# Attention in a hybrid trunk: the row maxima are turned four query tiles at a time and placed by VectorE, and the first pass is masked inside VectorE's maximum

## The reference, cut to what matters

```python
scale = q.shape[-1] ** -0.5
for blk in range(T // Q_BLOCK):
    lo, hi = blk * Q_BLOCK, (blk + 1) * Q_BLOCK
    s = jnp.einsum('bqhd,bkhd->bhqk', q[:, lo:hi], k[:, :hi]) * scale
    if log_decay_cum is not None:                      # fox only
        s = s + (cum[:, :, lo:hi, None] - cum[:, :, None, :hi])
    mask = (lo + jnp.arange(Q_BLOCK))[:, None] >= jnp.arange(hi)[None, :]
    p = jax.nn.softmax(jnp.where(mask, s, -jnp.inf), axis=-1)
    outs.append(jnp.einsum('bhqk,bkhd->bqhd', p, v[:, :hi]))
```

## Time and profile before

| what | value |
|---|---|
| median of 3 runs | 2560.76 us (2560.36 to 2562.09) |
| the profiled execution | 2564.89 us, of it span 2563.1 us |
| mean granted TensorE clock | 0.973 of full |
| TensorE matmuls busy | 2378.3 us (93%), 14804 |
| VectorE busy | 1163.1 us (45%), 1756 |
| ScalarE busy | 917.1 us (36%), 1508 |
| GpSimd busy | 792.6 us (31%), 740 |
| DMA | 141.33 MB, 54 GB/s over the span |

### The profile page before, as it was taken

The page is one execution under the profiler, slowest core; times in us unless marked ns, Lnnn a source line. Parts: engine busy times, 40 slices in busy tenths (PEclk is TensorE's granted clock), DMA queues, the critical chain, the costliest instruction groups (busy, mean ns, idle before and its releaser), DMA issues.

```text
span 2563.1 us, 35660 instructions
## 1 busy us (share of the span) xinstructions
PE 2378.3 (93%) x14804; PEld 1818.5 (71%) x14804; DVE 1163.1 (45%) x1756; ACT 917.1 (36%) x1508; POOL 792.6 (31%) x740
## 2 busy tenths in 40 slices
PE   7988999898999999899999889989999999998998
PEld 7867877885695876555696778778756858765556
DVE  4278144624335226565423872255342451266542
ACT  4332225513334333344332322263143243334341
POOL 1264211212514520354413532211134144203452
PEclk9989999999999999999998999999999999999999
DMA  4100331230100213100311003403201002131003
GB/s 145 53 18 2 93 121 38 99 115 1 34 17 1 64 38 115 58 1 1 133 67 53 18 1 99 148 6 133 81 1 34 17 1 64 37 115 58 1 1 123
DMA packets 91873, 141.33 MB, mean 55 GB/s; under 512 B 18208, under 2 KB 65344, under 8 KB 91712
## 3 DMA queue, kind: packets, MB, share of 16 engines
q1 hardware_dynamic: 91712, 139.05, 15.8%
HBM read 105.48 MB, written 33.55 MB: 54 GB/s over the span
## 4 chain that ended last, share of the span: by engine, by line
PE 77%; DVE 15%; ACT 3%; issue 2%; POOL 1%; DMA 1%; SPq 0%; POOLq 0%; DVEq 0%; ACTq 0%
PE psum L237 32%; PE psum L491 12%; PE psum L1379 6%; PE psum L1364 4%; PE psum L1333 4%; DVE gla_A L750 3%; PE psum L1365 3%; PE psum L1367 3%; PE psum L1346 2%; PE psum L1318 2%; PE psum L729 2%; PE psum L1386 1%; PE psum L981 1%; PE psum L1766 1%; DVE mla_nm L1514 1%
## 5 line engine op out<-in xcount | busy, mean ns | idle before, releaser
L196 POOL TENSOR_TENSOR w_lo<-w_raw,w_hi 128x2048 fp32r<-128x2048 f32 (+3 forms) x60 | 274.8, 4581 | 1013.0 <-ACT w_hi L189 1013.0
L237 PE MATMUL psum<-w_hi,h_hi 128*128 128x256 f32 (+3 forms) x1280 | 188.8, 291 | 20.7 <-ACT fox_k L1153 15.7
L237 PE MATMUL psum<-h_hi,w_hi 128*128 128x512 f32 x768 | 204.5, 410 | 0.0
L237 PE MATMUL psum<-h_lo,w_hi 128*128 128x512 f32 x768 | 198.8, 402 | 0.0
L1577 POOL TENSOR_TENSOR mla_acc<-mla_acc,mla_p 128x512 f32<-128x512 f32 (+3 forms) x160 | 164.5, 1043 | 109.6 <-ACT mla_p L1447 108.5
L237 PE MATMUL psum<-h_hi,w_lo 128*128 128x512 f32 x768 | 192.0, 392 | 0.0
L237 PEld LDWEIGHTS psum<-w_hi,h_hi 128*128 128x128 f32 x1280 | 169.5, 196 | 28.1 <-ACT fox_k L1153 16.5
L237 PE MATMUL psum<-w_lo,h_hi 128*128 128x256 f32 (+3 forms) x1280 | 180.8, 284 | 3.4 <-POOL w_lo L196 3.4
L237 PE MATMUL psum<-w_hi,h_lo 128*128 128x256 f32 (+3 forms) x1280 | 183.9, 288 | 0.0
L189 ACT ACTIVATE w_hi<-w_raw 128x2048 fp32r<-128x2048 f32 (+3 forms) x60 | 113.4, 1894 | 187.9 <-PE psum L491 172.8
L1577 POOL TENSOR_TENSOR fox_acc<-fox_acc,fox_p 128x512 f32<-128x512 f32 (+3 forms) x160 | 149.0, 950 | 91.0 <-ACT fox_p L1447 90.2
(11 more groups left out here) (318 smaller groups left out, 4504.4 us busy)
## 6 DMA issues: line engine op xcount, KB each, us to landing
w_raw<-in_w_in_dram SPq DMA_DIRECT2D x38, 1024.0 KB, 5.3
out_dram<-x_rows SPq DMA_DIRECT2D x64, 512.0 KB, 2.6
x_rows<-out_dram SPq DMA_DIRECT2D x56, 512.0 KB, 5.2
w_raw<-in_w_out_dram SPq DMA_DIRECT2D x16, 1024.0 KB, 6.6
x_first<-in_x_dram SPq DMA_DIRECT2D x8, 512.0 KB, 7.8
x_rows<-in_x_dram SPq DMA_DIRECT2D x8, 512.0 KB, 5.8
w_raw<-in_w_in_dram SPq DMA_DIRECT2D x2, 1088.0 KB, 9.1
w_raw<-in_w_in_dram SPq DMA_DIRECT2D x2, 1056.0 KB, 7.9
```

The lines of the kernel that those rows point to most:

```text
L196: pool.tensor_tensor(self.w_lo[c["set"]][:, :n], self.w_raw[c["set"]][:, :n], self.w_hi[c["set"]][:, :n].bitcast(F32), ALU.subtract).then_ ...
L237: last = pe.matmul(o, lhs, rhs, start=(kk == 0 and n == 0), stop=(kk == KT - 1 and n == 2))
```

## The change

Maxima: `turn_max` gives TensorE all four columns of maxima of a head as one stationary operand and turns them with one matmul into four rows of 128 (in fox with a fifth column of ones, for the decay row's place, because rows must begin at a multiple of 32). `place_max` moves from ScalarE to VectorE: one multiplication of these rows, repeated four times, by a 0/1 table `max_rows`, so that row r of `q_hi` holds the maxima of query tile r and zeros elsewhere. `k_hi` has ones in all of these rows. Contractions now go over 65 (fox) or 96 (mla) rows, and over 69 or 100 where the maxima take part; nothing has to be cleared any more. For `att0`, which shares the key tiles of `att1`, only the small tables are set.

Mask: the matmul L1335 goes. VectorE reduces the unmasked part of a diagonal tile, if there is one, and takes the last 128 keys with one `tensor_tensor_reduce` that adds the mask, scales by -1, writes the tile back to PSUM and gives the minimum. At the fourth query tile of each head, in shallow items too, a `tensor_reduce` joins up to three partial minima per query. `max_rows` is one more constant to load.

```diff
-M_ROW = 96
...
-NEG = -1e30
+NEG, KEEP = -1e30, 3e38
...
         self.rstd = self.at("norm_rstd", c + 4032, [P, TT])
+        self.max_rows = self.at("max_rows", c + 4064, [P, HH])
...
-        self.nm2 = k.at(f"{name}_nm2", small, [P, 2, 4, 2])
-        self.nmax = k.at(f"{name}_nmax", small + 64, [P, self.NI, 2, 4])
+        self.M = width // 32 * 32
+        self.R = width + HH
+        self.nm = k.at(f"{name}_nm", small, [P, 2, 2, HH, 3])
+        self.nmax = k.at(f"{name}_nmax", small + 192, [P, self.NI, 2, self.R - self.M])
...
-        n = {"blank": 2, "turned": G, "hi_done": G, "lo_done": G, "scores": T, "max_done": T, "max_joined": 2 * self.NP,
+        n = {"blank": 3 if keys_of is None else 1, "turned": G, "hi_done": G, "lo_done": G, "scores": T, "max_done": T, "max_joined": 2 * N,
...
-        diagonal = hi == (qt + 1) * P
-        last = pe.matmul(out, q[:M_ROW, a, x * P:(x + 1) * P], kk[:M_ROW, a, :hi - lo], start=True, stop=not diagonal)
-        if diagonal:
-            last = pe.matmul(out[:, hi - lo - P:], k.ident_bf[:, :], k.mask_bf[:, :], start=False, stop=True)
-        last.then_inc(self.scores.sem, 1)
+        pe.matmul(out, q[:D, a, x * P:(x + 1) * P], kk[:D, a, :hi - lo], start=True, stop=True).then_inc(self.scores.sem, 1)
...
     def turn_max(self, pe, i, a):
...
         self.misc_wait(pe, "m", i, a)
-        if self.items[i][1] == 0:
-            pe.wait_ge(self.max_done.sem, self.max_done.at(self.s_base[i] + 4 * (a + 1)))
-        else:
-            pe.wait_ge(self.max_joined.sem, self.max_joined.at(2 * (i // 2) + a + 1))
-        for x in range(4):
-            last = pe.matmul(k.psum[M_ROW:M_ROW + 1, self.misc_bank("m", i, a), x * P:(x + 1) * P],
-                             self.nmax[:, i, a, x:x + 1], k.ident[:, :], start=True, stop=True)
-        last.then_inc(self.m_turned.sem, 1)
+        pe.wait_ge(self.max_joined.sem, self.max_joined.at(2 * i + a + 1))
+        pe.matmul(k.psum[self.M:self.R, self.misc_bank("m", i, a), :P], self.nmax[:, i, a, :], k.ident[:, :], start=True,
+                  stop=True).then_inc(self.m_turned.sem, 1)
...
     def scores_turned(self, pe, i, j):
-        k, R = self.k, M_ROW + 1
+        k, D, R = self.k, self.width, self.R
...
-        pe.matmul(out, self.k_hi[ks][:M_ROW, a, keys], self.q_lo[qs][:M_ROW, a, lo:], start=False, stop=False)
+        pe.matmul(out, self.k_hi[ks][:D, a, keys], self.q_lo[qs][:D, a, lo:], start=False, stop=False)
...
-        last = pe.matmul(out, self.k_lo[ks][:M_ROW, a, keys], self.q_hi[qs][:M_ROW, a, lo:], start=False, stop=not diagonal)
+        last = pe.matmul(out, self.k_lo[ks][:D, a, keys], self.q_hi[qs][:D, a, lo:], start=False, stop=not diagonal)
...
     def round_group(self, act, p, g):
...
-        if p == 0 and g in (0, 4):
-            act.wait_ge(self.blank.sem, self.blank.at(1 + g // 4))
+        if self.keys_of is None and (p, g) in ((0, 0), (0, 4), (1, 0)):
+            act.wait_ge(self.blank.sem, self.blank.at(1 + 2 * p + g // 4))
...
-    def place_max(self, act, i, a):
-        p, c = self.items[i]
-        act.wait_ge(self.m_turned.sem, self.m_turned.at(2 * i + a + 1))
-        act.activation(self.q_hi[(2 * p + c) % self.QS][M_ROW:M_ROW + 1, a, :],
-                       self.k.psum[M_ROW:M_ROW + 1, self.misc_bank("m", i, a), :], ACT.Copy).then_inc(self.m_done.sem, 1)
...
             self.round_group(act, 0, g)
-        for a in range(2):
-            self.place_max(act, 0, a)
...
     def scalar(self, act, hook=None):
...
                     self.round_group(act, *self.pre_at(i, j))
-                if self.m_at(i, j) is not None:
-                    self.place_max(act, i + 1, self.m_at(i, j))
...
-    def blank_rows(self, dve, slots):
-        first = 64
-        for i in slots:
-            tiles = []
-            if self.width < M_ROW:
-                tiles = [self.q_hi[i], self.q_lo[i]]
-                if self.keys_of is None:
-                    tiles += [self.k_hi[i], self.k_lo[i]]
-            for x in tiles:
-                last = dve.memset(x[first:M_ROW, :, :].bitcast(F32), 0.0)
-            if self.keys_of is None:
-                last = dve.memset(self.k_hi[i][M_ROW:M_ROW + 1, :, :].bitcast(F32), 1.0)
+    def blank_rows(self, dve, i):
+        if i == 1:
+            last = dve.memset(self.nm[:, :, :, :, :], KEEP)
+            if self.M < self.width:
+                last = dve.memset(self.nmax[:, :, :, 0], 1.0)
+        if self.keys_of is None:
+            last = dve.memset(self.k_hi[i][self.M:self.R, :, :].bitcast(F32), 1.0)
...
     def maximum(self, dve, i, n):
-        c = self.items[i][1]
+        k, c = self.k, self.items[i][1]
...
         dve.wait_ge(self.scores.sem, self.scores.at(u + 1))
-        x = qt - 4 * c
-        if c and n % 8 == 0 and i >= 2:
-            dve.wait_ge(self.max_joined.sem, self.max_joined.at(2 * (i // 2 - 1) + a + 1))
-        out = self.nm2[:, a, x, part:part + 1] if c else self.nmax[:, i, a, x:x + 1]
-        dve.tensor_reduce(out, self.k.psum[:, 2 + u % 2, :hi - lo], AX_X, ALU.max, negate=True).then_inc(self.max_done.sem, 1)
-        if c and n % 8 == 7:
+        x, w = qt - 4 * c, hi - lo
+        ps = k.psum[:, 2 + u % 2, :]
+        if n % (4 * (c + 1)) == 0:
+            if i >= 2:
+                dve.wait_ge(self.max_joined.sem, self.max_joined.at(2 * (i - 2) + a + 1))
+            if a == 0 and i < 2:
+                dve.wait_ge(self.blank.sem, self.blank.at(2 if self.keys_of is None else 1))
+        nm = self.nm[:, c, a, x, :]
+        if part < c:
+            dve.tensor_reduce(nm[:, 0:1], ps, AX_X, ALU.max, negate=True).then_inc(self.max_done.sem, 1)
+            return
+        if w > P:
+            dve.tensor_reduce(nm[:, 1:2], ps[:, :w - P], AX_X, ALU.max, negate=True)
+        dve.tensor_tensor_reduce(ps[:, w - P:w], ps[:, w - P:w], k.mask_bf[:, :], -1.0, KEEP, ALU.add, ALU.min,
+                                 nm[:, 2:3]).then_inc(self.max_done.sem, 1)
+        if x == 3:
             dve.wait_ge(self.max_done.sem, self.max_done.at(u + 1))
-            dve.tensor_tensor(self.nmax[:, i, a, :], self.nm2[:, a, :, 0], self.nm2[:, a, :, 1], ALU.min)\
+            dve.tensor_reduce(self.nmax[:, i, a, self.width - self.M:], self.nm[:, c, a, :, :], AX_X, ALU.min)\
...
+    def place_max(self, dve, i, a):
+        p, c = self.items[i]
+        r, n = slice(self.M, self.R), self.R - self.M
+        dve.wait_ge(self.m_turned.sem, self.m_turned.at(2 * i + a + 1))
+        dve.tensor_tensor(self.q_hi[(2 * p + c) % self.QS][r, a, :].rearrange("r (x q) -> r x q", x=HH),
+                          self.k.psum[r, self.misc_bank("m", i, a), :P].unsqueeze(1).to_broadcast([n, HH, P]),
+                          self.k.max_rows[r, :].unsqueeze(2).to_broadcast([n, HH, P]), ALU.mult)\
+           .then_inc(self.m_done.sem, 1)
...
                 self.rest_of_group(dve, 0, groups[n // 2])
+        for a in range(2):
+            self.place_max(dve, 0, a)
...
     def vector(self, dve, hook=None):
...
                     self.maximum(dve, i + 1, n)
+                if self.m_at(i, j) is not None:
+                    self.place_max(dve, i + 1, self.m_at(i, j))
...
         self.loaded, self.angles, self.done, self.ones_set = (
-            Signal(k, n, c) for n, c in (("consts", 96), ("angles", 1), ("cos_done", 1), ("ones_set", 1)))
+            Signal(k, n, c) for n, c in (("consts", 112), ("angles", 1), ("cos_done", 1), ("ones_set", 1)))
...
     def load(self, sp):
...
+        sp.dma_start(k.max_rows[:, :], d["c_max_rows"]).then_inc(self.loaded.sem, 16)
...
     def wait_consts(self, eng):
-        eng.wait_ge(self.loaded.sem, self.loaded.at(96))
+        eng.wait_ge(self.loaded.sem, self.loaded.at(112))
...
-    a.att1.blank_rows(dve, (0,))
-    a.att1.blank_rows(dve, (1, 2))
+    for i in range(3):
+        a.att1.blank_rows(dve, i)
...
-    a.att0.blank_rows(dve, (0,))
-    a.att0.blank_rows(dve, (1, 2))
+    a.att0.blank_rows(dve, 1)
...
-    a.attC.blank_rows(dve, (0,))
+    a.attC.blank_rows(dve, 0)
...
     a.outB.add(dve, 1, 1)
-    a.attC.blank_rows(dve, (1, 2))
+    a.attC.blank_rows(dve, 1)
+    a.attC.blank_rows(dve, 2)
...
+    max_rows = np.zeros((P, HH), np.float32)
+    max_rows[HEAD] = 1.0
+    for first in (FOX_D, MLA_D):
+        max_rows[first:first + HH] = np.eye(HH)
...
+        "c_max_rows": max_rows,
```

## The result

The changed kernel takes 2670.21 us (median of 5 runs) against 2562.09 for the kernel before on the same chip: ratio 1.0413, 95% interval 1.0395 to 1.0432, **slower by 4.1%**, where I had forecast 2528.5 us and 0.90 for faster. A second job gave 2660.33 us, ratio 1.0353 (1.0317 to 1.0390); its profiled execution (2663.72 us) is read here. One run of each job (3016.35 and 2687.91 us) was in a slower state, at a lower clock than its neighbours, and stands outside the ratios.

What follows compares the result with a forecast made beforehand. TensorE was taken to bound deep items and VectorE's latency shallow ones. Terms -15.7, -17.2, -3.9, +2, +2 and +0.5 summed to -32.3 us, giving 2528.5 us against the median, range 2512 to 2549.

Steps and rivals of the forecast that it cites:

- part 2: TensorE's turns and masks: one turn for four, no mask matmuls, 2.25 us saved per deep item; fewer rows cost nothing.
- Part 6: Starts of the calls: +2 us for fox starts, +2 for half clock after mla's waits, +0.5 for the new constant.
- Part 1: Cleared rows in att1's start: fewer memsets end TensorE's 5.7 us idle and half clock after it, -15.7 us in all.
- Rival (d): The stall before att1's third transpose only moves to another wait: sum -16, 2544 us; chance 5%.
- Part 3: VectorE's prices: masked minimum 0.39 us, place 0.69, join 0.3; a diagonal tile costs 0.1 to 0.2 us more.
- Rival (a): The masked minimum on VectorE is dear: at 0.70 us the sum is zero, at 1.0 2593 us, slower; chance 10%.
- rival (c): More gained, 2513 us: no half clock in starts, minimum 0.28 us, join free of GpSimd contention; chance 9%.
- Part 4: Shallow items of fox end 0.5 to 1.45 us earlier; with the deep item -4.3 per fox call, -17.2 in all.
- Part 5: In mla, the place queued behind VectorE's hooks delays items by up to 3.9 us; net -1.95 per layer, -3.9 in all.
- Rival (b): mla's waits dearer by 2 to 4 us a call through lowered clock, starts too: 2539 to 2549 us; chance 14%.
- signs of being wrong: A masked minimum above 0.7 us, shallow items longer than before, or deep items with VectorE releasing the first-pass scores.
- signs of being right: Att1's third transpose without idle, at full clock; fox items 0, 1 at 15.6, 25.0 us; mla item 3 3-4 us late.

Runs made afterwards that it cites:

- b_rows: The kernel before with only the fox contractions' rows cut, 65 in place of 96 (the first matmul of the second pass keeps 97); 2629.0 us, ratio 1.0265.
- j_place: c_padded with four one-column turns and ScalarE's copy as before, leaving the mask part of the change alone; 2591.55 us, ratio 1.0113.
- c_padded: The changed kernel with fox contractions back at 96 and 100 rows and the spare rows cleared as before; 2612.36 us, ratio 1.0205.
- e_turns: c_padded with three further turns of the same maxima, results unused, for every head of every item; 2595.84 us, ratio 1.0131.
- h_start: c_padded with three further unused turns per head for item 0 alone, in the start of each call; 2577.19 us, ratio 1.0070.
- r_order: The kernel before with only the order changed: att1's cleared rows put between the groups; 2549.28 us, ratio 0.9958.
- k_order: h_start with att1's cleared rows put between the groups; 2560.23 us, ratio 0.9992.
- q_fox: p_128 without the early turn and with mla as in the kernel before, so the change in fox alone; 2539.58 us, ratio 0.9913.
- p_128: l_early with the second pass of fox over 128 rows; 2549.96 us, ratio 0.9964.
- l_early: k_order with a shallow item's second turn and place one unit earlier, unit 6 in place of 7; 2560.54 us, ratio 1.0015.

## Why the prediction was wrong

The step that failed is the last sentence of part 2, "The fewer rows of a contraction I cost at nothing: time goes with the columns in every row read." It is true of the busy time at one clock and false of the clock: by b_rows the rows alone cost 67 us. Two more steps failed beside it. Part 2 counted the masks and turns that go as time saved; at 96 rows the mask part alone is at +31 (j_place). Part 6 gave the clock +2 for waits in mla and counted the shorter turn phase of the starts as pure gain. That phase was what brought the clock back after the start's waits; without it item 0 of all six calls runs at half clock, five of them throughout. With the rows restored the whole is at +50 (c_padded): 31 for the masks, 4 more with the place on VectorE (e_turns; the two intervals overlap), 15 more with one turn in place of four. Three further turns in the starts alone take 35 of these away (h_start). +67 and +50 against the 98 us that the changed kernel lost in the same job: the two overlap, since an item can be at half clock only once.

Point by point, the terms that I did count:
- **Part 1** right. att1's starts are 8.6 and 7.3 us shorter, 15.9 against 15.7. The kernel before, with nothing but the order changed (r_order), gets 13.0 of them in the starts and 11 in its time. Rival (d) falls: nothing else holds the third transpose.
- **Part 2** nearly. A deep item takes 25.2 (fox) and 25.4 us (mla's item 5), so 2.1 and 1.9 against 2.25; of it 0.8 is the masks (j_place) where I had 0.95.
- **Part 3** right, on the high side. From the start of a masked minimum to the end of its read, where TensorE is released, it is 0.34 us against 0.39; the read starts 0.20 us in and holds nothing up, the next tile's reduction starts with it, so the 0.48 of a read that adds its whole length isn't reached. The place takes 0.69 as taken. Two tiles of att0's start:

```profile
797.51 0.28 DVE L1502 CUSTOM_DVE_ANT_0 psum<-psum,mask_bf 128x128 f32<-128x128 f32 x1
797.71 0.14 DVE L1502 DVE_READ_ACCUMULATOR2_ANT fox_nm<- 128x1 f32 x1
797.71 0.28 DVE L1501 TENSOR_REDUCE fox_nm<-psum 128x1 f32<-128x128 f32 x1
797.91 0.28 DVE L1502 CUSTOM_DVE_ANT_0 psum<-psum,mask_bf 128x128 f32<-128x128 f32 x1
```

  The Trainium skill's rule (VectorE: DVE Perf Modes, "Two Vector instructions with no wait between them") that an accumulator write is a second instruction agrees: 0.14 us, in rows of its own. Rival (a) falls. The join takes 0.17 us where I took 0.3. The 0.38 that I read was a mean of two kinds: in 22 of 32 the old join takes 0.16 us, and in the ten that begin while GpSimd multiplies two tiles (L1582) it takes 0.73 or 0.74 and ends 0.02 us after GpSimd does. In the kernel before:

```profile
1211.27 1.27 POOL L1582 TENSOR_TENSOR mla_gate<-mla_gate,mla_t 128x512 f32<-128x512 f32 x1 [0.63 <-DVE mla_t L1527]
1211.83 0.73 DVE L1517 TENSOR_TENSOR mla_nmax<-mla_nm 128x4 f32<-128x4 f32 x1
```

  The new join, a reduction, takes 0.17 in all 64, though 30 of them run beside GpSimd: the reason that rival (c) gave was right, and such a join is now 0.57 us shorter.
- **Part 4** right in sum, by luck in one term. h_start's att0: 15.3 + 25.2 + 17.2 + 20.0 = 77.7 against 82.0, -4.3 as forecast. Item 2 gained 1.3 and not 0.6 (the sum's figure; the text has 0.5 ahead of a last item), item 3 lost 0.65, which I had not counted.
- **Part 5** right in the waits, wrong in what they cost. TensorE's waits in the changed kernel (answer to the earlier trace rows):

```profile
1163.49 0.50 PE L1334 MATMUL psum<-mla_k_hi,mla_q_hi 96*128 96x512 f32 x1 [4.05 <-DVE mla_nm L1498]
...
1187.42 1.06 PE L1320 MATMUL psum<-ident,mla_q 128*96 128x128 f32 x4 [4.11 <-DVE mla_q L1626]
```

I had item 2's first maxima 3.2 us late; the wait is 4.05 where the kernel before shows 0.76 for the same instruction (1101.70 there). Layer 0's mla call lasts 213 us with its start in place of 204, 7 of them in item 0, by the start. k_order, whose item 0 is nearer to that of before, has the rest: its items 1 to 3 of mla take 84.3 and 87.0 us for 77.6, so +6.7 and +9.4 where I had +1.65 (3.9 less 2.25). Rival (b), half clock behind such waits, so came true at 5 and 8 us a call, beyond its 2 to 4. Item 3's transposes, which I had 3 to 4 us late against item 0, are 16 late in the changed kernel and 11 in k_order. k_order stands 21 us above q_fox; 12 of these are seen in the mla calls of the profiled executions, k_order's being its fastest of ten. j_place shows which part delays:

```profile
1115.78 0.50 PE L1333 MATMUL psum<-mla_k_hi,mla_q_hi 96*128 96x512 f32 x1 [1.45 <-DVE mla_nm L1512]
...
1140.59 0.68 PE L1319 MATMUL psum<-ident,mla_q 128*96 128x128 f32 x4 [2.71 <-DVE mla_q L1626]
```

With the place on ScalarE the second wait is the 2.71 of before and the first 1.45: the place on VectorE makes most of the lateness. It doesn't make all of the loss: j_place's items 1 to 3 still take 81.3 us for 77.6, with item 2 at a clock of 0.71 (k_order: 0.72).

The 0.5 us that part 6 gave the new constant isn't seen: TensorE's first work starts at 8.89 us in the changed kernel and at 8.92 in r_order, which doesn't load it. Of my signs of being wrong, "shallow items longer than before" came true. The signs of being right named "a full clock there" for att1's start only; it should have named the granted clock of every stage.

Open: what distinguishes a shallow item from a deep one for the clock, other than its records; what it is in the mask part that costs the clock; why item 2 of fox drops in e_turns and j_place and not in h_start, which works less; whether p_128 is ahead of l_early through its rows (their medians differ by 11 us and their intervals don't meet; in the profiled executions it is item 0 of two fox calls that drops in l_early alone); the level of h_start and k_order, above my expectation by more than mla's loss explains in their profiled executions.

## What to carry over

Read the granted clock by stage, and ask of each matmul that an edit removes or thins whether it kept that clock: 12 useless records ahead of item 0, 1.3 us at full clock, bought 3.6 to 8.9 us in each of six calls. Zero rows up to 96 in a contraction weren't waste here, although each column cost the same without them. Where one helper serves calls with different queues, try the change in each alone: in fox it was a gain once the rows and the starts' turns were kept, in mla a loss. And a mean duration can be of two kinds: read its least and its greatest (0.16 and 0.74 us in the old join).

## What the hardware showed that I had not expected

TensorE stayed at 1.2 GHz through 58 us in which it worked 57.18 (shown above), and through c_padded's 23.9 us with 22.86 of work, while in h_start a phase of turns that lasts 3.20 us had the clock back by its end. The Trainium skill (TensorE: Matmul & The Clock Gate, Part 1) has the gate follow how busy the engine has been; here busy time alone doesn't decide it, and the rows that a contraction uses, up to 96, do change it (67 us at 65 rows, 46 at 80).
